# Prompt attention of a hybrid decoder step: score products as three rounded products, sampled pages in four slots

## The chip, the core and the metric

One program runs on one core of a Trainium2 chip. The core has a matrix engine (PE; its weight loads are listed apart as PEld), a vector engine (DVE), a scalar engine (ACT), a third elementwise engine (POOL) and a queue that issues transfers (SP). Each engine works through its own list of instructions in order, and the lists meet only at semaphores. The metric is the time of one execution on the device in microseconds (us), as the median of several runs.

## What is computed

One layer of inference for a prompt of 1024 tokens and for 8 sampled sequences of 4 new tokens each, with 4096 past tokens in pages. The change lies in the attention of the prompt. Eight query heads of 64 numbers share two key heads (KVH = 2, four queries each), and every query is scored against three sets of keys:

```python
qg = q.reshape(B, Tq, N_KV_HEADS, GROUP, HEAD_DIM).astype(F32) * (HEAD_DIM ** -0.5)
s = jnp.einsum('btkgd,bnkd->bkgtn', qg, cmp_kv[:, :, 0]) - slopes * d_c.astype(F32)      # compressed
p_cmp = masked_softmax(s, d_c >= 0)
...
s = jnp.einsum('btkgd,bktmd->bkgtm', qg, ksel) - slopes * d_s.astype(F32)                # selected
...
s = jnp.einsum('btkgd,bskd->bkgts', qg, win_kv[:, :, 0].astype(F32)) - slopes * d_w.astype(F32)   # window
...
o = g[:, :, 0] * o_cmp + g[:, :, 1] * o_slc + g[:, :, 2] * o_win
```

With 1024 tokens all 16 blocks are selected, so the selected branch of the prompt is attention over all earlier keys.

## The kernel before

The program has a `front` (projections, convolution, compression of the cache) and, behind a barrier, the stages `attend`, `out_projection`, two MLP stages and an embedding stage. The change touches `attend` alone, from 525 to 866 us of the profiled execution.

**Units.** The prompt's attention is cut into 32 units, one for each of 4 query groups g and 8 blocks i of 128 queries (`UNITS[n] = (g, i)`, so i is n modulo 8). A unit's scores are products of `c.q[rows, g, ...]` (64 rows of one head, 128 queries) with 64 (compressed), 128(i+1) (selected) and 128(min(i,4)+1) (window) keys. `chunks_of` packs these pieces into chunks of at most 512 columns. For each piece two products are issued, for heads e = 0 and 1, that is on rows 0 to 63 and 64 to 127 of the array, and they write two banks (line 1895). Chunks of the first two units are already made in `front`.

**The path of a unit.** PE multiplies a chunk (L1895); DVE adds the distance penalty and takes the extreme of each row (L2156, one instruction for each piece and head, with a read of the accumulator behind it); ACT exponentiates (L2043); DVE inverts the sums (L2166, in `weigh`); POOL scales by that and by the gate (L1862, six instructions for a unit); PE turns the weights, 128 columns at a time (L1907); ACT and DVE by turns copy the turned banks (L2052, L2170); PE multiplies with the values (L1919); ACT copies a unit's output to `mixA` (`keep_o`, L2066).

**Order.** The orders of all engines are written out by hand over 88 steps of one to four per unit. In a step of unit n, PE turns two groups of unit n, then issues the share of unit n+2's chunks that falls in the step, then the value products of the step before, then work of the sampled queries, which runs in 18 quads: turning keys (L1946), their scores (`quad_scores`, L1954) and values (L1982). PE's products write two pairs of banks by turns (`score_banks`): a job waits until DVE has read the job two before it, and prompt chunks and quad scores count alike as jobs. In a unit's first step ACT's `keep_o(n - 1)` stands behind the exponentials of the step before; it waits for `pv_done`, the last value product of unit n-1, which PE issues behind this step's score products. DVE's first step of a unit is: copies of turned banks, then the scores of unit n+2's chunks, then the quad's scores; `weigh(n + 1)` stands in the second step, or in the first where a unit has one step (i = 0).

**Pages.** SP loads the sampled pages in 36 halves of 1 MB into five slots `s_raw`; half h waits until the values of quad (h - 5) // 2 are multiplied. The first weights of `out_projection` wait for the values of quad NZ - 3.

Of the kernel before, what the change touches and what calls it, by code (L numbers as in the profile page):

```python
# [14 lines left out]
ALU = mybir.AluOpType  # L15
ACT = mybir.ActivationFunctionType
# [6 lines left out]
P = 128  # L23
# [1619 lines left out]
EARLY_EXPS = 12  # L1643
RAW_PLACE = (AREA + 8192, RAW_OFF, HIY_OFF, HIY_OFF + 8192, AREA)


def attend(c, ps):
# [10 lines left out]

    raw = [c.at(f"s_raw{s}", [P, 8, 256], F32, RAW_PLACE[s]) for s in range(5)]
    KT_ = [c.at(f"s_KT{s}", [P, QK_], F32, PT_OFF + 8192 + 2048 * s) for s in range(4)]  # L1660
# [139 lines left out]
    iotas, step = c.sem("s_iotas"), c.sem("s_dve_step")  # L1800
    raw_loaded = [c.sem(f"s_raw_loaded{s}") for s in range(5)]
    cmp_ready, cmp_exp, imp_ready, selected = c.sem("s_cmp_max"), c.sem("s_cmp_exp"), c.sem("s_imp_ready"), c.sem("s_selected")
# [7 lines left out]
    def page(h, bb, j):  # L1810

        return raw[h % 5][:, 4 * (bb % 2) + j, :]

    def on_sp(sp):
        for h in range(2 * NZ):
            z = h // 2
            if h >= 5:
                sp.wait_ge(t_done, turn_no["o", (h - 5) // 2] + 1)
            for bb in (2 * (h % 2), 2 * (h % 2) + 1):
                b = GRP * group_of(z) + bb  # L1820
                if place(z) == 0:
                    sp.dma_start(raw[h % 5][:, 4 * (bb % 2):4 * (bb % 2) + 4, :], win[b]).then_inc(raw_loaded[h % 5], 16)
                else:
                    _, pages = nc.values_load_multi_w_load_instructions(
                        c.pages[0:1, ds(b * NPG + 4 * (place(z) - 1), 4)], engines=[mybir.EngineType.SP], min_val=0, max_val=N_POOL - 1)
                    for j in range(4):
                        sp.dma_start(page(h, bb, j), cache[ds(pages[j], 1)].rearrange("o t f -> (o t) f")).then_inc(raw_loaded[h % 5], 16)

# [39 lines left out]
    def on_pe(pe):  # L1868
# [17 lines left out]
        def qk(n, ch):  # L1886
            g, i = UNITS[n]
            s = score_banks(("p", n, ch))
            off = 0
            for br, k0, w in CHUNKS[n][ch]:  # L1890
                for e in range(KVH):
                    rows = slice(DH * e, DH * e + DH)
                    w0 = P * max(0, i - 4)
                    keys = c.KcP[rows, :] if br == 0 else c.proj[rows, KS, k0:k0 + w] if br == 1 else c.proj[rows, KW, w0 + k0:w0 + k0 + w]
# [136 lines left out]
    def on_act(act):  # L2031
# [36 lines left out]
        def quad_exps(z):  # L2068
# [54 lines left out]
    def on_dve(dve):  # L2123
# [118 lines left out]
        def keep_out(gr):  # L2242
# [1562 lines left out]
```

## Time and profile before

| | us |
|---|---|
| median of 3 runs | 1786.9 (1786.52 to 1790.64) |
| the profiled execution, its own time | 1786.75 |
| its span in the trace | 1785.1 |
| stage `attend` within it | 525 to 866 |

PE is busy for 1729.3 us of the span, and in every other stage it is close to fully busy. In `attend` its work is in short bursts of four kinds, with idle gaps between them. A busy PE is not PE at its peak, since products are pipelined: what a burst costs is read from the start of one burst to the start of the next. The granted clock of PE is at its upper level (2.4 GHz) over nearly the whole span; a window that prints 0.50 had the lower one (1.2 GHz).

### The profile page before, as it was taken

What the parts mean: (1) busy time and instruction counts of PE and PEld (TensorE: products, weight loads), DVE (VectorE), ACT (ScalarE), POOL (GpSimd) and SP (SyncE); (2) the same over time, 40 slices, a digit from 0 to 9 for tenths busy, and PEclk for the clock granted to TensorE, in tenths of its full rate; (3) what the DMA queues carried; (4) which work ended last, traced back from release to release, by engine and by line L of the source; (5) the groups of instructions that cost most, each with busy time, mean ns of one, the idle gap of its engine ahead of it and who ended that gap; (6) DMA issues with size and microseconds to landing.
All of it is one profiled execution on the core that took longest, in us unless ns stands there. A gap on an engine that the chain in (4) does not pass through costs nothing.

```text
span 1785.1 us, 36056 instructions
## 1 busy us (share of the span) xinstructions
PE 1729.3 (97%) x13587; PEld 1603.5 (90%) x13587; DVE 1215.0 (68%) x1813; ACT 803.4 (45%) x1458; POOL 844.0 (47%) x862
## 2 busy tenths in 40 slices
PE   8999999999989999999998899999999999999998
PEld 7999999999876766676998899999999999999998
DVE  6789964878677677767647645555587878855535
ACT  5312323555766566666525233333443333314426
POOL 2203964545524343344444656566665555325531
PEclk9999997999999999999999999999999999999999
DMA  4421356545522544343314233222393733431214
GB/s 160 131 72 38 95 161 155 149 142 148 179 71 82 149 121 127 109 136 90 134 36 151 84 112 117 97 109 97 132 312 122 216 113 107 146 112 55 59 36 145
DMA packets 179723, 214.61 MB, mean 120 GB/s; under 512 B 22940, under 2 KB 150664, under 8 KB 174799
## 3 DMA queue, kind: packets, MB, share of 16 engines
q1 hardware_dynamic: 174461, 196.82, 35.5%
q0 software_dynamic: 4032, 13.40, 2.4%
q10 hardware_dynamic: 1058, 2.10, 0.4%
q8 instruction: 108, 1.77, 0.4%
q14 instruction: 64, 0.52, 0.1%
HBM read 181.30 MB, written 35.59 MB: 121 GB/s over the span
## 4 chain that ended last, share of the span: by engine, by line
PE 55%; DVE 8%; issue 3%; POOL 2%; ACT 2%; DMA 0%; ACTq 0%; SPq 0%; DVEq 0%; POOLq 0%
PE ps L2740 11%; PE ps L3123 7%; PE ps L2745 6%; PE ps L2500 5%; PE ps L3128 4%; PE ps L200 3%; PE ps L1907 3%; PE ps L3636 3%; PE ps L1919 3%; PE ps L1895 3%; POOL S L1862 2%; PE ps L1946 2%; DVE S L2156 2%; PE ps L206 2%; PE ps L3646 1%
## 5 line engine op out<-in xcount | busy, mean ns | idle before, releaser
L1862 POOL TENSOR_SCALAR S<-S,inv,gate_p 128x640 f32<-128x640 f32 (+7 forms) x186 | 124.9, 691 | 193.7 <-DVE inv L2166 193.7
L1260 DVE SCALAR_TENSOR_TENSOR y<-u,conv_w,y 128x1024 f32<-128x1024 f32 x120 | 156.4, 1349 | 1.2
L3123 PE MATMUL ps<-dn_op_hi,dn_hi 128*128 128x264 f32 x672 | 136.5, 285 | 2.9 <-DVE dn_op_lo L3171 2.9
L3123 PE MATMUL ps<-dn_op_lo,dn_hi 128*128 128x264 f32 x672 | 135.7, 283 | 0.0
L636 POOL COPY relaid<-raw 128x512 f32<-128x512 f32 x128 | 82.3, 675 | 94.9 <-PE ps_p L1034 35.6
L2043 ACT ACTIVATE S<-S,mn 128x64 f32<-128x64 f32 (+8 forms) x180 | 108.7, 609 | 2.1 <-DVE mn L2156 2.1
L3054 POOL TENSOR_TENSOR dn_lo<-dn_t_sum,dn_hi 128x512 fp32r<-128x512 f32 x48 | 76.4, 1592 | 66.7 <-ACT dn_hi L3076 66.5
L2740 PE MATMUL ps<-s_hi,up_hi 128*128 128x264 f32 x512 | 104.8, 286 | 3.0 <-ACT rstd L2710 3.0
L3123 PEld LDWEIGHTS ps<-dn_op_hi,dn_hi 128*128 128x128 f32 x672 | 103.7, 188 | 4.2 <-DVE dn_op_lo L3171 4.2
L963 PE MATMUL ps_p<-Ahi,win_hi 128*128 128x352 f32 x456 | 103.8, 327 | 1.5 <-DVE Alo L1237 1.5
L2740 PE MATMUL ps<-s_lo,up_hi 128*128 128x264 f32 x512 | 104.5, 286 | 0.0
L3123 PEld LDWEIGHTS ps<-dn_op_lo,dn_hi 128*128 128x128 f32 x672 | 103.9, 188 | 0.0
L963 PE MATMUL ps_p<-Alo,win_hi 128*128 128x352 f32 x456 | 103.5, 326 | 0.0
L1907 PEld LDWEIGHTS ps<-ident,S 128*128 128x128 f32 x592 | 64.9, 142 | 38.9 <-issue 21.0
L1907 PE MATMUL ps<-ident,S 128*128 128x128 f32 x592 | 86.4, 283 | 12.4 <-POOL S L1862 8.6
L1108 PE MATMUL ps_p<-Xhi,w1hi 128*128 128x256 f32 (+1 forms) x288 | 95.8, 333 | 1.0 <-ACT gT L772 0.8
L3128 PE MATMUL ps<-dn_op_hi,dn_lo 128*128 128x264 f32 x672 | 95.6, 284 | 0.0
L2610 POOL TENSOR_TENSOR up_lo<-up_sum,up_hi 128x512 fp32r<-128x512 f32 x48 | 70.5, 1469 | 46.6 <-ACT up_hi L2656 46.6
L3128 PEld LDWEIGHTS ps<-dn_op_hi,dn_lo 128*128 128x128 f32 x672 | 87.7, 188 | 0.0
L1110 PE MATMUL ps_p<-Xhi,w1lo 128*128 128x256 f32 (+1 forms) x288 | 84.7, 294 | 0.0
L1109 PE MATMUL ps_p<-Xlo,w1hi 128*128 128x256 f32 (+1 forms) x288 | 84.6, 294 | 0.0
L2740 PE MATMUL ps<-a_hi,up_hi 128*128 128x264 f32 x384 | 79.0, 288 | 5.6 <-DVE tmp L2817 3.5
(484 smaller groups left out, 5073.9 us busy)
## 6 DMA issues: line engine op xcount, KB each, us to landing
s_raw<-in_cache_slc_kv_dram SPq DMA_DIRECT2D x256, 128.0 KB, 2.1
raw<-in_cache_cmp_kv_dram SPq DMA_DIRECT2D x192, 128.0 KB, 3.1
dn_op_raw<-hidden SPq DMA_DIRECT2D x21, 1056.0 KB, 6.7
hidden<-cs SPq DMA_DIRECT2D x32, 528.0 KB, 2.6
up_raw<-in_w_up_dram SPq DMA_DIRECT2D x16, 1024.0 KB, 5.3
dn_w<-in_w_down_dram SPq DMA_DIRECT2D x48, 256.0 KB, 4.9
win_raw<-in_w_in_dram SPq DMA_DIRECT2D x38, 256.0 KB, 3.3
raw<-in_cache_cmp_kv_dram POOLq DMA_DIRECT2D x64, 128.0 KB, 2.6
```

Source lines behind the costliest of these rows:

```text
L963: mm = nc.tensor.matmul(ps[t % 2][:, j, 0:CH], w[t % 2][:, k, :], x[:, k, CH * j:CH * j + CH], start=(m == 0), stop=(m == NG - 1))
L1108: nc.tensor.matmul(out, w1hi[cc][:, at, :], x_hi, start=first, stop=False)
L1110: mm = nc.tensor.matmul(out, w1lo[cc][:, at, :], x_hi, start=False, stop=last)
L1260: i = V_.scalar_tensor_tensor(out=y, in0=x, scalar=w, in1=y, op0=ALU.mult, op1=ALU.add)
L1862: nc.gpsimd.tensor_scalar(x, x, inv[:, n % 3, 3 * e + br:3 * e + br + 1], c.gate_p[:, i, H * br + h:H * br + h + 1], ALU.mult, ALU.mult).t ...
L1907: mm = nc.tensor.transpose(ps[:, P * (2 * j + e):P * (2 * j + e) + P], S[UNITS[n][1]][:, e, col:col + P], c.ident[:])
L2043: nc.scalar.activation(x, x, ACT.Exp, bias=mn[:, n % 3, e, br, part:part + 1], scale=-1.0, accum_out=sums[:, n % 3, 3 * e + br:3 * e + br ...
L2500: mm = nc.tensor.matmul(banks[t % 2][:, j, 0:CH], w[t % 2][:, k, :], x(k)[:, CH * j:CH * j + CH], start=(n == 0 and m == 0), stop=(n == KT ...
L2740: nc.tensor.matmul(ps[:, bank + j, 0:HC], w_hi[s % 4][:, k, :], ops[m][:, k, c0 + HC * j:c0 + HC * j + HC], start=(k == 0 and m == 0), sto ...
L2745: mm = nc.tensor.matmul(ps[:, bank + j, 0:HC], w_lo[s % 4][:, k, :], ops[0][:, k, c0 + HC * j:c0 + HC * j + HC], start=False, stop=(k == K ...
L3123: nc.tensor.matmul(ps[:, 2 * m + j, 0:HC], w_hi[q % 4][:, k, :], x[:, k, HC * j:HC * j + HC], start=(k == 0 and x is op_hi[n]), stop=False)
L3128: mm = nc.tensor.matmul(ps[:, 2 * m + j, 0:HC], w_lo[q % 4][:, k, :], op_hi[n][:, k, HC * j:HC * j + HC], start=False, stop=(k == KH - 1))
```

## The change

Queries, keys and compressed keys are split into a part rounded to the format fp32r (`hi`, a copy on ACT) and the rest (`lo`, a subtraction on DVE). Each score piece becomes three products that add up in the bank, hi by hi, hi by lo and lo by hi, in place of one product of fp32 numbers. The keys are split at the start of the stage, in two parts cut at column 384. Queries are split unit by unit: unit 2's at the start, and in the first step of unit n those of unit n+3. `K_hi` takes the place of the fifth page slot, so there are four: half h waits for the values of quad (h - 4) // 2, and the weights of `out_projection` for quad NZ - 2.

```diff
-RAW_PLACE = (AREA + 8192, RAW_OFF, HIY_OFF, HIY_OFF + 8192, AREA)
+RAW_SLOTS = 4
+RAW_PLACE = (HIY_OFF, RAW_OFF, HIY_OFF + 8192, AREA + 8192)
+KEY_CUT = 384
...
+    K_hi = c.at("K_hi", [P, 2, T], F32R, AREA)
+    K_lo = c.at("K_lo", [P, 2, R], F32R, PROJ_OFF + 4 * R * KS)
+    KcP_hi = c.at("KcP_hi", [P, 64], F32R, RSTD_OFF + 4096)
+    KcP_lo = c.at("KcP_lo", [P, 64], F32R, B1_OFF + 15616)
+    q_lo = c.at("q_lo", [P, PAIRS, R], F32R, U_OFF)
+    q_hi = [sb("q_hi0", [P, P], F32R), c.at("s_q_hi1", [P, P], F32R, RSTD_OFF + 3584)]
+    query_part = lambda n: 1 if n == 2 else n + 2
...
-            if h >= 5:
-                sp.wait_ge(t_done, turn_no["o", (h - 5) // 2] + 1)
+            if h >= RAW_SLOTS:
+                sp.wait_ge(t_done, turn_no["o", (h - RAW_SLOTS) // 2] + 1)
...
+            if ch == 0:
+                pe.wait_ge(part_lo, 3 if n == 2 else query_part(n))
+            w0 = P * max(0, i - 4)
+            hi, lo = q_hi[n % 2], q_lo[query(n)]
             for br, k0, w in CHUNKS[n][ch]:
-                for e in range(KVH):
-                    rows = slice(DH * e, DH * e + DH)
-                    ...
-                    mm = nc.tensor.matmul(ps_S[:, s + e, off:off + w], c.q[rows, g, P * i:P * i + P], keys, start=True, stop=True)
+                for m, (x, split, compressed) in enumerate(((hi, K_hi, KcP_hi), (hi, K_lo, KcP_lo), (lo, K_hi, KcP_hi))):
+                    for e in range(KVH):
+                        rows = slice(DH * e, DH * e + DH)
+                        mm = nc.tensor.matmul(ps_S[:, s + e, off:off + w], x[rows, :], keys(rows, split, compressed), start=(m == 0), stop=(m == 2))
...
+        def query_high(n):
+            if n >= 4:
+                act.wait_ge(qk_done, score_no["p", n - 2, len(CHUNKS[n - 2]) - 1] + 1 - len(EARLY))
+            nc.scalar.activation(q_hi[n % 2][:], c.q[query(n)], ACT.Copy).then_inc(part_hi, 1)
+        query_high(2)
+        nc.scalar.activation(K_hi[:, :, KEY_PARTS[0]], c.proj[:, KS:KW + 1, KEY_PARTS[0]], ACT.Copy).then_inc(part_hi, 1)
...
                 if j == 0 and n:
                     keep_o(n - 1)
+                if j == 0 and n + 3 < NU:
+                    query_high(n + 3)
...
-                    if k == 0:
-                        act.wait_ge(t_done, turn_no["o", NZ - 2] + 1)
+                    if k < 2:
+                        act.wait_ge(t_done, turn_no["o", NZ - 2 + k] + 1)
...
+        def query_low(n):
+            dve.wait_ge(part_hi, query_part(n))
+            V_.tensor_tensor(q_lo[query(n)], c.q[query(n)], q_hi[n % 2][:].bitcast(F32), ALU.subtract).then_inc(part_lo, 1)
...
                 z = quad_at(st, 1)
                 if z is not None:
                     keep_keys(z, 3)
+                if j == 0 and n + 3 < NU:
+                    query_low(n + 3)
...
-    c.t_done, c.slot_free = t_done, turn_no["o", NZ - 3] + 1
+    c.t_done, c.slot_free = t_done, turn_no["o", NZ - 2] + 1
```

The changed file's lines stand some 30 further down. DVE in the first step of unit 12, before: a copy of a turned bank and of keys, then unit 14's scores (`S_10086`) and the quad's (`s_S`).

```order
L2170 COPY PT_10091<-ps 128x512
L2173 COPY s_KT_10101<-ps 128x512
L2156 ISA S_10086,mn<-ps,far_selected,neg_slope 128x512
...
L2156 ISA S_10086,mn<-ps,far_selected,mn,neg_slope 128x384
...
L2156 ISA S_10086,mn<-ps,far_compressed,neg_slope 128x64
L2156 ISA mn 128x1
L2207 ISA s_S_10102,s_mx<-ps,s_S_10102,s_mx 128x512
```

The same place after the change:

```order
L2202 COPY PT_10091<-ps 128x512
L2205 COPY s_KT_10105<-ps 128x512
L2285 TENSOR_TENSOR q_lo<-q_back,s_q_hi_10132 128x128
L2188 ISA S_10086,mn<-ps,far_selected,neg_slope 128x512
L2188 ISA mn 128x1
...
L2239 ISA s_S_10106,s_mx<-ps,s_S_10106,s_mx 128x512
```

The subtraction for unit 15's queries has moved in ahead of unit 14's scores. It waits for this row of ACT's list, `s_q_hi`, which stands behind the output copy `mixA` (`keep_o`) of the same step:

```order
L2064 ACTIVATE S_10085,sums<-S_10085,mn 128x640 x2
L2087 ACTIVATE mixA<-ps 128x128
L2104 ACTIVATE s_q_hi_10132<-q_back 128x128
L2073 ACTIVATE PT_10088<-ps 128x512
L2098 ACTIVATE s_alpha<-s_mx,s_nm,row_slope 128x1
```

In unit 8, whose only step also holds `weigh(9)`, the subtraction stands ahead of the inversion as well:

```order
L2202 COPY PT_10089<-ps 128x256
L2205 COPY s_KT_10105<-ps 128x512
L2285 TENSOR_TENSOR q_lo<-q_back,s_q_hi_10132 128x128
L2198 RECIPROCAL inv<-sums 128x6
L2188 ISA S_10082,mn<-ps,far_selected,neg_slope 128x384
```

PE's list has, for the first chunk of unit 2 with 384 and 64 columns, six products where there were two for each piece:

```order
L1916 MATMUL ps<-K_hi,q_lo 128x384 x2
L1916 MATMUL ps<-KcP_hi,s_q_hi_10131 128x64 x2
L1916 MATMUL ps<-KcP_lo,s_q_hi_10131 128x64 x2
L1916 MATMUL ps<-KcP_hi,q_lo 128x64 x2
L1916 MATMUL ps<-K_hi,s_q_hi_10131 128x384 x2
```

These rows are its last product with selected keys, its three with compressed ones and the first of the next chunk; each "x2" is the two heads.

## Rows read from the trace of the kernel before

**Rows 1.** Stage attend by window: start:end, length, busy us (count), clock, DMA.
```profile
525.00:866.00 341.00, 322.73 (x3464) 228.49 (x3466) 242.23 (x806) 219.49 (x600) 146.96 (x217) 0.99 0.40 119
```

**Rows 2.** Line L1895: ns min/median/max, first and last start, forms and counts.
```profile
L1895 PE MATMUL ps<-proj,q_back x368: 269/538/1006, 526.5 to 847.2; 64*128 64x512 f32 x80, 64*128 64x128 f32 x44, 64*128 64x384 f32 x32, 64*128 64x256 f32 x28
L1895 PE MATMUL ps<-KcP,q_back x120: 216/272/418, 527.9 to 847.3; 64*128 64x64 f32 x120
```

**Rows 3.** Timeline, bursts on PE and weight loads: start, us, engine, line, shapes, count.
```profile
646.32 1.13 PE L1895 MATMUL ps<-proj,q_back 64*128 64x512 f32 x4
647.38 1.09 PE L1919 MATMUL ps<-PT,V 128*64 128x128 f32 x16
...
663.58 1.99 PE L1895 MATMUL ps<-proj,q_back 64*128 64x512 f32 x8
665.50 0.66 PE L1919 MATMUL ps<-PT,V 128*64 128x128 f32 x8
...
642.89 0.92 PE L1895 MATMUL ps<-proj,q_back 64*128 64x256 f32 x8
643.92 1.09 PE L1919 MATMUL ps<-PT,V 128*64 128x128 f32 x16
...
664.12 0.19 PEld L1895 LDWEIGHTS ps<-proj,q_back 64*128 64x128 f32 x2 [0.24 <-issue]
```

**Rows 4.** Timeline, rounded products of front, 132 columns wide.
```profile
264.05 0.28 PE L1108 MATMUL ps_p<-Xhi,w1hi 128*128 128x132 f32 x1
264.16 0.27 PE L1109 MATMUL ps_p<-Xlo,w1hi 128*128 128x132 f32 x1
```

**Rows 5.** Timeline, unit 12's first step (brackets: idle before it, releaser).
```profile
653.73 0.28 ACT L2066 ACTIVATE mixA<-ps 128x128 f32<-128x128 f32 x1 [0.47 <-PE ps L1919]
...
654.03 1.06 PE L1954 MATMUL ps<-s_KT,QB 128*32 128x512 f32 x8 [0.35 <-DVE mn L2156]
```

**Rows 6.** Timeline, unit 9.
```profile
625.61 0.26 ACT L2066 ACTIVATE mixA<-ps 128x128 f32<-128x128 f32 x1
...
625.80 0.19 DVE L2166 RECIPROCAL inv<-sums 128x6 f32<-128x6 f32 x1 [0.42 <-ACT S L2043]
...
626.10 3.36 POOL L1862 TENSOR_SCALAR S<-S,inv,gate_p 128x384 f32<-128x384 f32 x6 [5.65 <-DVE inv L2166]
```

**Rows 7.** Timeline, unit 16.
```profile
706.35 0.18 DVE L2166 RECIPROCAL inv<-sums 128x6 f32<-128x6 f32 x1
...
707.39 0.28 ACT L2066 ACTIVATE mixA<-ps 128x128 f32<-128x128 f32 x1 [0.74 <-PE ps L1919]
```

**Rows 8.** Timeline, unit 13 (its third job starts at the second row).
```profile
666.42 0.28 ACT L2066 ACTIVATE mixA<-ps 128x128 f32<-128x128 f32 x1 [0.96 <-PE ps L1919]
...
667.33 1.13 PE L1895 MATMUL ps<-proj,q_back 64*128 64x512 f32 x4
```

**Rows 9.** Groups by form in attend: busy us, mean ns of one, idle before it.
```profile
L2156 DVE CUSTOM_DVE_ANT_0 S<-ps,far_selected,neg_slope 128x512 f32<-128x512 f32 x40 | 28.4, 748 | 11.0 <-PE ps L1895 10.9
...
L2066 ACT ACTIVATE mixA<-ps 128x128 f32<-128x128 f32 x31 | 8.4, 270 | 14.3 <-PE ps L1919 14.3
L2112 ACT ACTIVATE y_hi<-y 128x1056 fp32r<-128x1056 f32 x4 | 4.3, 1076 | 0.0
L2295 DVE TENSOR_TENSOR y_lo<-y,y_hi 128x1056 fp32r<-128x1056 f32 x4 | 5.3, 1328 | 0.2 <-ACT y_hi L2112 0.2
```

**Rows 10.** Timeline at the start of the stage: PE's wait for DVE.
```profile
530.12 0.62 PE L1930 MATMUL ps<-KcS,QB 128*32 128x256 f32 x2 [0.59 <-DVE mn L2156]
```

**Rows 11.** Window with half the clock, a burst of turns in it, and another elsewhere.
```profile
551.00:553.00 2.00, 2.00 (x10) 1.72 (x9) 0.29 (x1) 1.29 (x3) 0.69 (x2) 0.50 0.00 0
...
551.21 1.91 PE L1946 MATMUL ps<-ident,s_raw 128*128 128x128 f32 x8
...
631.60 1.09 PE L1946 MATMUL ps<-ident,s_raw 128*128 128x128 f32 x8
```

**Rows 12.** Timeline, pages issued on SP's queue.
```profile
599.82 10.46 SPq L1827 DMA_DIRECT2D s_raw<-in_cache_slc_kv_dram  x12
```

More of the change, by code:

```diff
@@ L1657, in attend @@
     LOW = 1e20
-    raw = [c.at(f"s_raw{s}", [P, 8, 256], F32, RAW_PLACE[s]) for s in range(5)]
+    raw = [c.at(f"s_raw{s}", [P, 8, 256], F32, RAW_PLACE[s]) for s in range(RAW_SLOTS)]
+    K_hi = c.at("K_hi", [P, 2, T], F32R, AREA)
[3 more added lines that the diff above has]
+    q_lo = c.at("q_lo", [P, PAIRS, R], F32R, U_OFF)
     KT_ = [c.at(f"s_KT{s}", [P, QK_], F32, PT_OFF + 8192 + 2048 * s) for s in range(4)]
@@ L1793, in attend @@
     HALF_DMAS = lambda h: 2 if place(h // 2) == 0 else 8
-    arrived = lambda h: 16 * sum(HALF_DMAS(x) for x in range(h % 5, h + 1, 5))
+    arrived = lambda h: 16 * sum(HALF_DMAS(x) for x in range(h % RAW_SLOTS, h + 1, RAW_SLOTS))
     qk_done, score_read = c.sem("qk_done"), c.sem("score_read")
@@ L1800, in attend, with query @@
     iotas, step = c.sem("s_iotas"), c.sem("s_dve_step")
-    raw_loaded = [c.sem(f"s_raw_loaded{s}") for s in range(5)]
+    raw_loaded = [c.sem(f"s_raw_loaded{s}") for s in range(RAW_SLOTS)]
+    part_hi, part_lo = c.sem("key_or_query_hi_ready"), c.sem("key_or_query_lo_ready")
+    query_part = lambda n: 1 if n == 2 else n + 2
+    KEY_PARTS = (slice(0, KEY_CUT), slice(KEY_CUT, T))
+    def query(n):
+        g, i = UNITS[n]
+        return (slice(None), g, slice(P * i, P * i + P))
     cmp_ready, cmp_exp, imp_ready, selected = c.sem("s_cmp_max"), c.sem("s_cmp_exp"), c.sem("s_imp_ready"), c.sem("s_selected")
@@ L1810, in page @@
     def page(h, bb, j):
-        return raw[h % 5][:, 4 * (bb % 2) + j, :]
+        return raw[h % RAW_SLOTS][:, 4 * (bb % 2) + j, :]
     def on_sp(sp):
@@ L1826, in on_sp @@
                     for j in range(4):
-                        sp.dma_start(page(h, bb, j), cache[ds(pages[j], 1)].rearrange("o t f -> (o t) f")).then_inc(raw_loaded[h % 5], 16)
+                        sp.dma_start(page(h, bb, j), cache[ds(pages[j], 1)].rearrange("o t f -> (o t) f")).then_inc(raw_loaded[h % RAW_SLOTS], 16)
     def on_pool(pool):
@@ L1889, in qk, with keys @@
             off = 0
+            if ch == 0:
+                pe.wait_ge(part_lo, 3 if n == 2 else query_part(n))
+            w0 = P * max(0, i - 4)
+            hi, lo = q_hi[n % 2], q_lo[query(n)]
             for br, k0, w in CHUNKS[n][ch]:
-                for e in range(KVH):
-                    rows = slice(DH * e, DH * e + DH)
-                    w0 = P * max(0, i - 4)
-                    keys = c.KcP[rows, :] if br == 0 else c.proj[rows, KS, k0:k0 + w] if br == 1 else c.proj[rows, KW, w0 + k0:w0 + k0 + w]
-                    mm = nc.tensor.matmul(ps_S[:, s + e, off:off + w], c.q[rows, g, P * i:P * i + P], keys, start=True, stop=True)
+                def keys(rows, split, compressed):
+                    return compressed[rows, :] if br == 0 else split[rows, 0, k0:k0 + w] if br == 1 else split[rows, 1, w0 + k0:w0 + k0 + w]
+                for m, (x, split, compressed) in enumerate(((hi, K_hi, KcP_hi), (hi, K_lo, KcP_lo), (lo, K_hi, KcP_hi))):
+                    for e in range(KVH):
+                        rows = slice(DH * e, DH * e + DH)
+                        mm = nc.tensor.matmul(ps_S[:, s + e, off:off + w], x[rows, :], keys(rows, split, compressed), start=(m == 0), stop=(m == 2))
                 off += w
@@ L1941, in turn_keys @@
             h = 2 * z + half
-            pe.wait_ge(raw_loaded[h % 5], arrived(h))
+            pe.wait_ge(raw_loaded[h % RAW_SLOTS], arrived(h))
             for bb in (2 * half, 2 * half + 1):
@@ L2078, in quad_exps @@
             nc.scalar.activation(Ss[z % 2][:], Ss[z % 2][:], ACT.Exp, bias=shift, scale=slope, accum_out=part_sum[:, z % 2, 0:1]).then_inc(sx_done, 1)
+        def query_high(n):
[4 more added lines that the diff above has]
+        nc.scalar.activation(K_hi[:, :, KEY_PARTS[0]], c.proj[:, KS:KW + 1, KEY_PARTS[0]], ACT.Copy).then_inc(part_hi, 1)
+        nc.scalar.activation(KcP_hi[:], c.KcP[:], ACT.Copy).then_inc(part_hi, 1)
+        nc.scalar.activation(K_hi[:, :, KEY_PARTS[1]], c.proj[:, KS:KW + 1, KEY_PARTS[1]], ACT.Copy).then_inc(part_hi, 1)
         late = []
@@ L2249, in keep_out @@
             o.then_inc(kept[1], 1)
+        def query_low(n):
+            dve.wait_ge(part_hi, query_part(n))
+            V_.tensor_tensor(q_lo[query(n)], c.q[query(n)], q_hi[n % 2][:].bitcast(F32), ALU.subtract).then_inc(part_lo, 1)
+        query_low(2)
+        dve.wait_ge(part_hi, 2)
+        V_.tensor_tensor(K_lo[:, :, KEY_PARTS[0]], c.proj[:, KS:KW + 1, KEY_PARTS[0]], K_hi[:, :, KEY_PARTS[0]].bitcast(F32), ALU.subtract).then_inc(part_lo, 1)
+        dve.wait_ge(part_hi, 3)
+        V_.tensor_tensor(KcP_lo[:], c.KcP[:], KcP_hi[:].bitcast(F32), ALU.subtract).then_inc(part_lo, 1)
+        dve.wait_ge(part_hi, 4)
+        V_.tensor_tensor(K_lo[:, :, KEY_PARTS[1]], c.proj[:, KS:KW + 1, KEY_PARTS[1]], K_hi[:, :, KEY_PARTS[1]].bitcast(F32), ALU.subtract).then_inc(part_lo, 1)
         dve.wait_ge(iotas, 7)
```

2 lines of the change are left out of this document (1 added, 1 removed).

## The prediction, made before the changed kernel had run

> **What bounds the kernel now.** I read the windows first, by stages. PE is near full everywhere, and in attend it is busy for 322.73 of 341 us, DVE for 242, ACT for 219, POOL for 147 [rows 1]. So a microsecond of PE's work taken away in attend is worth nearly one, as long as PE doesn't then wait for somebody. The idle 18.3 us of PE shows that it already waits: the timeline has PE held by DVE's reading of scores [rows 5] and POOL by DVE's inversion [rows 6]. The stage is a loop through all engines, and what matters next to PE's work is how soon DVE reads a unit's scores.
>
> **What the products cost.** The line of the score products has 488 records, four for each piece (two heads, two passes of an fp32 product); by the forms there are 40 pieces of 512 columns, 16 of 384, 14 of 256, 22 of 128 and 30 of 64 [rows 2]. One chunk of 512 takes PE from 646.32 to 647.38, 1.06 us; two in a row take from 663.58 to 665.50, 1.92 us. So 512 columns cost 0.86 us and the burst as such 0.20 us. 0.86 us is 2048 periods of 2.4 GHz, four a column for both heads together: four records stream 1024 periods each, so the two heads run at the same time, and so do their weight loads (two in 0.19 us, the time of one) [rows 3]. A chunk of 256, 128 and 64 columns takes 1.03 us, 0.83 without the burst; 384 columns are 0.64 of that, so the 64 columns are about 0.17 [rows 3].
>
> **What three rounded products cost.** The fp32 pass streams two periods a column. Rounded products of 132 columns, each with its own load of 128 columns of weights, start 0.11 us apart, though 132 periods are 0.055 us [rows 4]. So I take for a pass of both heads the larger of one period a column and 0.107 us. Three passes then cost 0.64 us for 512 columns (saves 0.21), 0.48 for 384 (0.16), 0.32 for 256 (0.11), 0.32 for 128 (before 0.21, loses 0.11) and 0.32 for 64 (before 0.17, loses 0.15). Sum: 40 x 0.21 + 16 x 0.16 + 14 x 0.11 - 22 x 0.11 - 30 x 0.15 = 8.4 + 2.6 + 1.5 - 2.4 - 4.5 = **5.6 us saved on PE**; I write 6, as a 64-column piece may load its first weights under the piece before. The bound above is that loads hide wholly: 34944 columns less one period each of four, 14.6 us, some 13 with a few ns per product. The bound below is the rival of serial heads.
>
> The Trainium skill, FP8 and Floating Point Precision, TensorE Precision Notes, says that a true fp32 product makes four passes through the array. The trace's four periods a column agree. By that rule alone three passes for four would save the whole 14.6 us; the rows on short rounded products speak against it, and by them 6.
>
> **What is moved, and who waits.** 28 queries are split unit by unit. The copy on ACT and the subtraction on DVE are short: an ACT copy of 128 columns takes 0.27 us, and DVE needs 1.33 us for 1056 columns, so 0.16 us in proportion and up to 0.3 with a fixed share; I take 0.25 [rows 9]. In all some 8 us more on ACT and 7 us on DVE, beside a stage of 341 us in which neither is full: by itself nothing.
>
> Their place is what costs. In a unit's first step ACT rounds the query behind `keep_o(n - 1)`, which waits for PE's last value product of unit n-1; that stands on PE behind this step's score products. DVE's `query_low(n + 3)` waits for ACT, and queued behind it on DVE are the reading of the scores just multiplied, in the one-step units also the inversion for the next unit. Nothing needs q_lo(n+3) before the next unit: the wait serves nobody, but it holds DVE until 0.28 + 0.27 + 0.25 = 0.80 us after the start of `keep_o`. For `keep_o` the trace has 14.3 us of idle time ended by PE in 31 copies: it follows the value product directly in many of them, else the exponentials of the step before [rows 9]. Before, DVE reads scores as soon as the chunk is multiplied, mostly 1.5 to 3 us sooner.
>
> I went through the 28 starts of units in the timeline, adding 0.80 us to `keep_o` and 0.71 us for each 512-column piece and head (28.4 us for 40) [rows 9], up to the first thing on PE that needs it:
> - *Five starts with a quad's scores in the step* (units 8, 12, 18, 20, 26). The quad's product needs the bank of the job two before it. Unit 12: DVE is free at 653.73 + 0.80 = 654.53, has read the first chunk at 655.95, and PE's product started at 654.03 [rows 5]: 1.9 us. Five make 10.
> - *Four second units of a query group* (1, 9, 17, 25), where two chunks of 512 lie between the split and the inversion. Unit 9: 625.61 + 0.80 + 4 x 0.71 = 629.25, and the inversion was at 625.80, with POOL idle 5.65 us for it and PE's turning right behind [rows 6]: 3.4. The four make 2.9 + 3.4 + 1.1 + 3.0 = 10.4.
> - *Two one-step units* (16, 24). Unit 16: the inversion stood at 706.35 and comes at 707.39 + 0.80 = 708.19 [rows 7]: 1.8. Together 4.
> - *Nine starts in which PE's third job or a bank of turned blocks comes too late* (2, 5, 6, 10, 13, 14, 21, 22, 28). Unit 13: 666.42 + 0.80 + 1.42 = 668.64 against 667.33 [rows 8]: 1.3. By the same reckoning these are 0.2 to 2.7 each, together 15.
> - *The other eight* (3, 4, 7, 11, 15, 19, 23, 27) have other work on PE or short scores: 3.
>
> Sum 42 us. Some of it falls into gaps that PE has already: of its 18.3 us idle [rows 1] I take 10 off, **32 us** for this term. Its bounds are 21 (half of the sum, if DVE and ACT catch up and the stalls of neighbours overlap) and 42.
>
> **The start of the stage.** Before PE's first score product ACT now rounds a query, 768 columns of keys and 64 compressed ones (0.27 + 0.8 + 0.2 us, the keys by proportion of 1.08 us for 1056), and DVE subtracts (1.0 + 0.15 behind it) [rows 9]; the second key part of 1280 columns adds 1.3 us on ACT and 1.6 on DVE ahead of their first copies and the first scores. DVE reads them about 1.4 us later than now, and PE's product at 530.12 already waits for DVE [rows 10]. With the lower clock held a little longer: **2 us**.
>
> **Clock.** At 551.00:553.00 the granted clock was 0.50, the lower level, and a burst of eight turns took 1.91 us, against 1.09 us for such a burst elsewhere [rows 11]. New pauses of 2 to 3 us may bring more such stretches. I take none into the sum and 5 us (six at 0.8) into the upper bound. The Trainium skill, TensorE: Matmul & The Clock Gate, HAM oscillation, says that idle gaps between bursts bring the lower clock back, which speaks against this change; by that row such a stretch costs 0.8 us a burst.
>
> **Slots.** The even half of a quad's pages now starts a quad later. Twelve transfers take SP 10.46 us [rows 12], so the 16 of a quad 14 us, the first eight 7; between the values that free the slots and the turning of the keys lie 4 to 6 steps of 3.9 us (341 for 88). The first half has 15 us or more for 7, the second 19 for 14: hidden. If transfers took twice as long it would be late by some 7 us a quad.
>
> **Sum.** 1786.75 (the profiled execution, 0.15 under the median of 1786.9, so no correction) + 32 + 2 - 6 = 1814.75: **1815 us**, 1.6% slower.
>
> **The rivals.**
> - *Faster: the wait is hidden and PE's saving stays.* It decides whether PE's other work between the last value product and the next consumer of a bank (turning, keys, sampled values) is longer than 0.80 us plus the reading, 2.2 us. It is in unit 15 and a few more, not in units 8, 9 or 12. If it were nearly everywhere, 1786.75 + 2 - 6 to - 13: 1776 to 1783, middle 1781. For it: DVE is idle for 99 of 341 us. Against it: the rows of units 9, 12 and 13.
> - *Nothing measurable.* Stalls of a third of the sum, 14 us, with the full saving of 13 and 2 for the start: about 1788.
> - *Heads in turn.* No row shows rounded products on half the rows. If the two heads' products did not run together, a pass would cost twice: six periods a column instead of four, 34944 x 2 / 2.4 GHz = 29 us more instead of 6 less. With the stalls partly covered: 1840 to 1850. For it: nothing but the missing row; against: the fp32 products on the same halves do overlap [rows 3].
>
> **How the numbers follow.** Chances: the forecast 0.70, heads in turn 0.12, nothing measurable 0.08, faster 0.10. A measurement of this kernel can tell about 0.3% (5.4 us) from no change. Faster by more 0.10, within 0.08, slower 0.82. The forecast's own bounds: 1786.75 + 21 + 1 - 13 = 1796, and 1786.75 + 42 + 2 + 5 - 0 = 1836. Taking in part of the washed-out case below and of heads in turn above, the range is 1790 to 1842; outside are the faster case and small parts of the two.
>
> **What would show it.** After the change: bursts of 512 columns on PE of about 0.85 us, not 1.06 (the saving) and not 1.5 (heads in turn); 64- and 128-column pieces no faster than before. On DVE the new subtraction as one of the largest waits, ended by ACT, 28 times for 1 to 3 us, and PE's idle time for DVE's reads and POOL up from 18 to 40 us or more in a stage of some 370 us; everything behind the stage as before. The forecast is wrong if DVE's subtraction waits less than 0.5 us on average, or if PE's idle time in the stage stays near 18 us.

## The result, and the profile after

| | before | after |
|---|---|---|
| median | 1787.4 us (1786.5 to 1790.6, 4 runs) | 1839.5 us (1837.1 to 1844.7, 4 runs) |
| ratio, 95% interval | | 1.0287 (1.0263 to 1.0312) |
| the profiled execution | 1786.75 | 1839.03 |
| first score product of the stage, in its span | 526.47 | 529.78 |
| first product of `out_projection` | 866.50 | 917.64 |

The change makes the kernel 2.9% slower, by 52 us. 1815 was predicted, 28 us more than before, with 1790 to 1842 around it. The two windows between those points, of before and of after (columns: length, then busy time and instruction count of PE, PEld, DVE, ACT and POOL, the granted clock, the share of the DMA engines and GB/s):

```profile
526.47:866.50 340.03, 321.79 (x3466) 227.68 (x3465) 242.73 (x806) 219.67 (x600) 146.06 (x209) 0.99 0.40 120
```

```profile
529.78:917.64 387.86, 335.80 (x3708) 254.13 (x3708) 247.25 (x836) 225.98 (x629) 146.59 (x209) 0.94 0.35 105
```

The stage takes 47.8 us more. PE's idle time in it, length less busy, goes from 18.2 to 52.1 us (+33.8), and PE's busy time rises by 14.0 us although the products were to become cheaper. Of the 52.3 us by which the spans differ, 3.3 lie before the first score product and 1.2 behind the stage. Counted from PE's first product of the stage (525.03 before, 527.42 after), 2.4 of the 3.3 lie ahead of the stage and 0.9 in it: the first score product comes 2.36 us behind that product instead of 1.44, since it waits for the split of the keys:

```profile
529.78 0.69 PE L1916 MATMUL ps<-K_hi,s_q_hi 64*128 64x384 f32 x2 [0.84 <-DVE KcP_lo L2291]
```

**The wait.** From the list of waits of after (engine and line, what it waited for, us in total, times, longest):

```profile
POOL S L1878 <- DVE inv L2198: 241.0, 30, 12.5
ACT PT L2073 <- PE ps L1928: 105.2, 59, 8.0
DVE q_lo L2285 <- ACT s_q_hi L2104: 70.7, 29, 5.2
```

DVE's new subtraction waits 70.7 us for ACT's copy. PE's part of the list has no such line; there the same wait appears as waits for `mn`, what DVE's readings of scores write, for `s_KT`, DVE's copies of keys, and for POOL:

```profile
PE ps L1928 <- POOL S L1878: 14.0, 15, 2.2
PE ps L1975 <- DVE mn L2188: 11.4, 5, 2.5
PE ps L1916 <- DVE mn L2188: 9.4, 8, 2.0
PE ps L1967 <- DVE s_KT L2205: 5.8, 4, 3.0
```

Before, PE waited 8.6 us for POOL in the first of these lines, 1.8 us in the second, none in the third and 1.1 us in the fourth.

The timeline of unit 12 shows the whole chain (start, duration, engine, line, output<-input, idle time before it and what ended it), the place of [rows 5]:

```profile
678.30 0.44 PE L1940 MATMUL ps<-PT,VcP 128*64 128x128 f32 x4
...
678.78 0.28 ACT L2087 ACTIVATE mixA<-ps 128x128 f32<-128x128 f32 x1 [0.27 <-PE ps L1940]
678.96 0.30 ACT L2104 ACTIVATE s_q_hi<-q_back 128x128 fp32r<-128x128 f32 x1
679.29 0.29 DVE L2285 TENSOR_TENSOR q_lo<-q_back,s_q_hi 128x128 fp32r<-128x128 f32 x1 [1.87 <-ACT s_q_hi L2104]
679.50 0.75 DVE L2188 CUSTOM_DVE_ANT_0 S<-ps,far_selected,neg_slope 128x512 f32<-128x512 f32 x1
...
680.98 1.06 PE L1975 MATMUL ps<-s_KT,QB 128*32 128x512 f32 x8 [2.24 <-DVE mn L2188]
```

PE ends its value products, ACT copies the output and then rounds the query, DVE subtracts, and only then reads the first 512 columns twice; PE's next product waits for the second reading, 2.24 us.

**The bursts.** The same piece of 512 columns as in [rows 3], now in three passes, from the first row to the start of the next kind of work:

```profile
683.00 0.50 PE L1916 MATMUL ps<-K_hi,s_q_hi 64*128 64x512 f32 x2
683.34 0.40 PE L1916 MATMUL ps<-K_lo,s_q_hi 64*128 64x512 f32 x2
683.57 0.41 PE L1916 MATMUL ps<-K_hi,q_lo 64*128 64x512 f32 x2
683.90 1.09 PE L1940 MATMUL ps<-PT,V 128*64 128x128 f32 x16
```

0.90 us instead of 1.06. By size, at full clock: 512 columns 1.06 to 0.89, two of 512 1.92 to 1.59, 384 0.85 to 0.72, 256 0.63 to 0.55, but 128 0.42 to 0.48 and 64 0.37 to 0.45.

**The clock.** The granted clock falls to its lower level, 1.2 GHz, much more often. This is the row behind PE's pause of unit 16, and the two-us windows there (the clock stands third from the end):

```profile
740.62 2.18 PE L1928 MATMUL ps<-ident,S 128*128 128x128 f32 x8 [2.19 <-POOL S L1878]
```

```profile
738.00:740.00 2.00, 0.42 (x8) 0.18 (x4) 1.02 (x5) 0.47 (x2) 0.53 (x1) 1.00 0.79 234
740.00:742.00 2.00, 1.26 (x6) 0.87 (x7) 2.00 (x11) 0.40 (x1) 2.00 (x6) 0.71 0.35 90
742.00:744.00 2.00, 2.00 (x10) 1.47 (x10) 1.90 (x6) 2.00 (x10) 1.38 (x3) 0.50 0.69 201
744.00:746.00 2.00, 2.00 (x22) 1.32 (x21) 0.92 (x2) 1.32 (x6) 0.00 (x0) 0.94 0.00 0
```

Summed over all such windows from 524 on (2 us for one at 0.50, in proportion for the others) the lower level holds for 51 us, against 8.5 before. Of that, 47 and 6 lie behind the first score product.

### The profile page after: what moved, and what is told of

Read it like the earlier page. It is cut to its first block, busy times and chain, and to the rows that moved or that the text cites. A ratio compares the mean times of both kernels' runs of the same rounds, so it can differ in the third digit from the quotient of the medians.

```text
span 1837.4 us, 36639 instructions
## 1 busy us (share of the span) xinstructions
PE 1745.4 (95%) x13831; PEld 1631.5 (89%) x13831; DVE 1222.5 (67%) x1846; ACT 811.4 (44%) x1491; POOL 843.7 (46%) x862
## 4 chain that ended last, share of the span: by engine, by line
PE 48%; DVE 10%; issue 5%; ACT 4%; POOL 2%; DMA 1%; SPq 0%; ACTq 0%; DVEq 0%; POOLq 0%
PE ps L2785 11%; PE ps L3168 6%; PE ps L2790 5%; PE ps L2545 4%; PE ps L3173 3%; PE ps L200 3%; PE ps L1928 2%; PE ps L1916 2%; PE ps L1940 2%; DVE S L2188 2%; PE ps L3681 2%; POOL S L1878 2%; PE ps L206 1%; DVE dn_op_lo L3216 1%; ACT S L2064 1%
## 5 line engine op out<-in xcount | busy, mean ns | idle before, releaser
L1928 PE MATMUL ps<-ident,S 128*128 128x128 f32 x592 | 91.4, 294 | 20.2 <-POOL S L1878 14.0
L2073 ACT ACTIVATE PT<-ps 128x512 f32<-128x512 f32 (+1 forms) x80 | 45.0, 562 | 105.4 <-PE ps L1928 105.2
```

What stands on the lines that cost most here:

```text
L1928: mm = nc.tensor.transpose(ps[:, P * (2 * j + e):P * (2 * j + e) + P], S[UNITS[n][1]][:, e, col:col + P], c.ident[:])
```

## The experiments

For each profile the table gives the stage from its first score product to the first product of `out_projection`, PE's busy and idle time in it, and the time at the lower clock, summed from 2-us windows from 524 on. These four columns are of one execution each; medians and ratios are of all. Ratios are to the kernel before on the same chip.

| kernel | median, us | ratio (95%) | stage | busy | idle | lower clock |
|---|---|---|---|---|---|---|
| before | 1787.4 | 1 | 340.0 | 321.8 | 18.2 | 8.5 |
| after | 1839.5 | 1.0287 (1.0263 to 1.0312) | 387.9 | 335.8 | 52.1 | 51.1 |
| e4_four_slots | 1790.8 | 1.0010 (0.9997 to 1.0023) | 340.3 | 322.1 | 18.3 | 10.2 |
| e3_wait_alone | 1838.8 | 1.0272 (1.0245 to 1.0300) | 391.5 | 340.2 | 51.4 | 47.8 |
| e1_split_early | 1790.3 | 1.0012 (1.0001 to 1.0023) | 339.5 | 319.9 | 19.7 | 17.1 |
| e2_subtraction_late | 1792.1 | 1.0019 (1.0010 to 1.0029) | 341.1 | 320.0 | 21.1 | 17.1 |
| e7_copy_early | 1788.7 | 1.0011 (1.0000 to 1.0022) | 338.9 | 318.5 | 20.3 | 12.0 |
| e5_pauses_filled | 1834.2 | 1.0257 (1.0236 to 1.0277) | 380.6 | 336.6 | 44.0 | 27.3 |
| e8_two_products | 1783.8 (one run) | not timed | 329.7 | 300.0 | 29.6 | 17.1 |
| e6_compressed_fp32 | 1791.0 | 1.0009 (0.9999 to 1.0019) | 339.9 | 316.6 | 23.3 | 16.8 |
| e9_keys_later | 1791.8 | 1.0014 (1.0004 to 1.0023) | 342.4 | 318.4 | 24.0 | 13.7 |
| e10_both | 1791.8 | 1.0012 (1.0001 to 1.0022) | 339.5 | 315.1 | 24.4 | 13.4 |

The first score product starts anywhere from 525.5 to 532.3 in these profiles, though the code ahead of the stage is the same in all. So of the 3.3 us by which it is later in the profile of after only the 0.9 within the stage say something of the change. They stand in every version that splits all keys at the start (2.36 us from PE's first product of the stage to its first score product), and are absent in e4_four_slots and e3_wait_alone (1.44). The column "stage" leaves them out. With them, from PE's first product of the stage to the first of `out_projection`, it is 341.5 us before, 390.2 after, 341.8 in e4_four_slots and 341.9 in e1_split_early.

### The two parts of the change apart: the slots, and the wait

e4_four_slots, from the kernel before:

```diff
-RAW_PLACE = (AREA + 8192, RAW_OFF, HIY_OFF, HIY_OFF + 8192, AREA)
+RAW_SLOTS = 4
+RAW_PLACE = (HIY_OFF, RAW_OFF, HIY_OFF + 8192, AREA + 8192)
```

e3_wait_alone, from e4_four_slots, with the copy on ACT and the subtraction on DVE where the changed kernel has them:

```diff
                 if j == 0 and n:
                     keep_o(n - 1)
+                if j == 0 and n + 3 < NU:
+                    query_high(n + 3)
...
                     keep_keys(z, 3)
+                if j == 0 and n + 3 < NU:
+                    query_low(n + 3)
```

> The kernel before with the sampled pages in four slots, and nothing else of the change. My theory: the loads are hidden, 1785 to 1789 us, no wait of PE's turning of keys over 1 us in the stage. Rival (the first half of a quad comes late by a part of the 2.4 us of the front or by some us a quad): 1790 or more, with PE's key turning waiting for the queue.

> The kernel before, with its fp32 products and unsplit keys, with four slots and with the 28 query copies on ACT and subtractions on DVE in the places of the changed kernel; their results are read by nobody. My theory: the wait alone brings pauses and clock, so the time is that of the changed kernel with 5 us more on PE and without the longer start: 1786.75 + 35 + 20 = 1830 to 1848, PE idle 48 to 56 us in the stage, 40 us or more at the lower clock, DVE's subtraction waiting 60 to 80 us. Rival (the clock falls because of the rounded products): 1786.75 + 35 = about 1822, with under 15 us at the lower clock. Second rival (the wait is not the cause): 1787 to 1795.

Four slots cost nothing that can be told: the ratio's interval holds 1, and the stage is 0.3 us longer (the median is above the 1785 to 1789 that I gave, but so was that of the kernel before beside it, 1789.2). The wait alone, with the old products, gives the whole loss: 1.0272 against 1.0287, with intervals that overlap. Its time, idle time, lower clock and waits all lie in what was expected. The few us by which the old products are dearer don't show in the medians; its four executions lie between 1834 and 1841 us. From the waits of e3_wait_alone:

```profile
DVE q_lo_unused L2269 <- ACT s_q_hi L2092: 73.5, 28, 4.8
```

The stages of e4_four_slots and of e3_wait_alone, same columns as above:

```profile
529.20:869.53 340.33, 322.06 (x3466) 227.08 (x3465) 242.82 (x806) 219.62 (x600) 146.10 (x209) 0.99 0.40 120
```

```profile
528.33:919.86 391.53, 340.18 (x3466) 235.33 (x3465) 245.32 (x835) 226.47 (x629) 145.38 (x209) 0.94 0.35 104
```

PE executes the same 3466 instructions in both. Idle time rises by 33.1 us, and the same work takes 18.1 us longer, with 37.6 us more at the lower clock: 0.48 us for each. Together 51.2 us. So the lower clock comes with the pauses and not from rounded products, of which this kernel has none in its scores; nor from the split of the keys, which it doesn't have either.

### Without the wait

e1_split_early, from the changed kernel, on ACT (the line goes to the head of the step) and on DVE (it goes to the end of the step):

```diff
+                if j == 0 and n + 3 < NU:
+                    query_high(n + 3)
                 for k in steps[st]:
...
                 if j == 0 and n:
                     keep_o(n - 1)
-                if j == 0 and n + 3 < NU:
-                    query_high(n + 3)
...
-                if j == 0 and n + 3 < NU:
-                    query_low(n + 3)
...
+                if j == 0 and n + 3 < NU:
+                    query_low(n + 3)
```

> The changed kernel with the query's copy at the head of ACT's step (ahead of the exponentials and keep_o) and the subtraction at the end of DVE's step (behind the readings of scores); the products, keys and slots are as changed. My theory (the wait of DVE's subtraction for the copy is what costs: 35 us of pauses on PE, and some 20 us of lower clock that follow the pauses): DVE's subtraction waits under 3 us in all instead of 70.7, PE's idle time in the stage is 18 to 22 us instead of 53, the time at the lower clock falls from 50 to 10 to 15 us, and the kernel takes 1783 to 1791 us. Rival (the rounded products themselves, or the split of the keys, bring the lower clock; the wait costs only its own pauses): 1839 less 35 = 1804, with 40 us or more still at the lower clock. Second rival (four slots or the work of the split hold PE): over 1815.

e2_subtraction_late moves the line on DVE alone, e7_copy_early the one on ACT alone.

> The changed kernel with one line moved: DVE's subtraction of the query stands at the end of DVE's step, behind the readings of scores; ACT's copy stays behind keep_o. My theory (what costs is only what is queued behind the waiting subtraction on DVE): as e1_split_early, 1786 to 1793, with DVE's subtraction waiting under 5 us. Rival (ACT's copy behind keep_o itself delays ACT's next exponentials, which PE's turning needs): 1795 to 1805.

> The changed kernel with the other line moved alone: ACT's copy of the query stands at the head of ACT's step, ahead of the exponentials and keep_o; DVE's subtraction stays ahead of the readings of scores. My theory (the wait is for keep_o, which waits for PE's last value product): DVE waits for ACT only where ACT is late by its exponentials, under 15 us in all, and the kernel takes 1787 to 1797. Rival (DVE would wait at that place for whatever ACT has in hand, so half of the cost stays): 1805 to 1820, with 30 us or more of waits.

Each of the three takes the loss away. The place of unit 12 in e1_split_early:

```profile
651.24 0.30 ACT L2104 ACTIVATE s_q_hi<-q_back 128x128 fp32r<-128x128 f32 x1
654.03 0.75 DVE L2188 CUSTOM_DVE_ANT_0 S<-ps,far_selected,neg_slope 128x512 f32<-128x512 f32 x1 [0.21 <-PE ps L1916]
...
655.17 0.28 ACT L2087 ACTIVATE mixA<-ps 128x128 f32<-128x128 f32 x1 [0.27 <-PE ps L1940]
...
655.51 1.06 PE L1975 MATMUL ps<-s_KT,QB 128*32 128x512 f32 x8 [0.39 <-DVE mn L2188]
```

DVE reads the scores 1.1 us before the output copy instead of 0.7 behind it, and PE's pause is 0.39 us, not 2.24. PE's idle time of 19.7 us in the stage lies in the range told, the time at the lower clock of 17.1 us a little above it. DVE's subtraction waits for ACT 1.9 us in all here. With either line moved alone it is (e2_subtraction_late, where under 5 us was expected, then e7_copy_early):

```profile
DVE q_lo L2285 <- ACT s_q_hi L2104: 6.1, 7, 1.9
```

```profile
DVE q_lo L2285 <- ACT s_q_hi L2104: 2.7, 3, 1.9
```

Both rivals fell: the copy behind `keep_o` by itself delays nothing much, and DVE doesn't wait for whatever else ACT has in hand. It was the dependence on `keep_o`, that is on PE, and what stood behind it on DVE.

But none of the three beats the kernel before; all lie 0.1 to 0.2% above it, within what I called no change. The stage of e1_split_early:

```profile
528.41:867.95 339.54, 319.87 (x3709) 245.46 (x3709) 250.19 (x836) 225.55 (x629) 146.50 (x209) 0.98 0.40 120
```

Against e4_four_slots PE is busy 2.2 us less, with 6.9 us more at the lower clock, at 0.48 each 3.3 us: the products save 5.5 us, of which 3.3 go to the lower clock and 1.4 into idle time. The lower clock lies in the first stretch of the stage in both, up to 552 here and up to 557 there. The 0.8 us that are left are used up by the first score product, which comes 0.9 us later: nothing reaches the end of the stage.

### Is the lower clock caused by the pauses?

```diff
 e5_pauses_filled, from the changed kernel
+FILLED = (1, 8, 10, 12, 16, 18, 20, 21, 24, 26)
...
                 for k in (steps[st - 1] if st else ()):
                     pv(k)
+                if j == 0 and n in FILLED:
+                    pe.wait_ge(o_kept, n)
+                    nc.tensor.matmul(ps_O[:, 0:512], c.ident[:], c.Tslc[:, 0:512], start=True, stop=True)
```

> The changed kernel with one fp32 product of 512 columns more on PE (0.86 us, read by nobody) behind the last value product and keep_o in ten of the units, those where PE then pauses for 2 us or more. It separates the pauses' own length from the lower clock that follows them. My theory (the clock falls behind long pauses, and a pause cut in two keeps it): the time at the lower clock falls from 50 to 25 to 35 us (what the start and the stretch at 545 to 560 hold stays), and the kernel takes 8 to 12 us less than the changed one less up to 4 us for the fillers: 1829 to 1836. Rival (the clock follows how much PE has to do over a longer stretch, so single fillers change nothing): 1839 to 1848, with 45 us or more at the lower clock.

Ten products of which nobody reads anything make the kernel 5 us faster by the medians; the intervals of the two ratios still overlap (the executions lie at 1832.5 to 1837.8 and at 1837.1 to 1844.7). The stage, one execution of each, is 380.6 us against 387.9. Unit 16 again, PE's rows and then the windows, to be held against the four windows of after above:

```profile
738.16 1.13 PE L2034 MATMUL ps<-far_selected,ident 128*128 128x512 f32 x2 [0.38 <-ACT mixA L2091]
739.98 0.66 PE L1929 MATMUL ps<-ident,S 128*128 128x128 f32 x4 [0.69 <-POOL S L1879]
741.05 0.66 PE L1929 MATMUL ps<-ident,S 128*128 128x128 f32 x4 [0.42 <-POOL S L1879]
```

```profile
738.00:740.00 2.00, 1.15 (x3) 0.32 (x3) 1.66 (x9) 0.30 (x2) 1.17 (x3) 1.00 0.63 199
740.00:742.00 2.00, 1.58 (x12) 1.13 (x14) 1.93 (x9) 1.33 (x4) 2.00 (x5) 1.00 0.47 137
742.00:744.00 2.00, 2.00 (x24) 1.36 (x20) 1.97 (x5) 2.00 (x9) 0.75 (x1) 1.00 0.38 125
```

One pause of 2.19 us has become three of 0.38, 0.69 and 0.42, and the clock stays at 1.00. Over the stage the time at the lower clock falls from 51.1 to 27.3 us; this and the time of the kernel lie in what was expected. Busy time rises by 0.8 us, though the fillers take 11.3, so the other work takes 10.5 less; 23.8 us times 0.48 is 11.4. Idle time falls by 8.1 us, since the fillers lie in it. A filler shortens a pause and gives PE more to do at once, so this run doesn't tell which of the two keeps the clock up. What is left at the lower clock is the start, 528 to 542, and stretches at 552 to 562 and 648 to 651.

The Trainium skill, TensorE: Matmul & The Clock Gate, HAM oscillation, says that idle gaps between bursts send the clock back, so that the next burst starts at the lower one. These two runs agree: the same work takes 18.1 us longer in e3_wait_alone, and all but the fillers 10.5 us less in e5_pauses_filled. The page's example is one of waits for DMA; here it was pauses of 2.0 to 3.0 us, in which PE waited for DVE and POOL.

### What a pass costs, and what PE's time is worth

e8_two_products is e1_split_early without the third product, so its scores lack the low part of the query.

```diff
-                for m, (x, split, compressed) in enumerate(((hi, K_hi, KcP_hi), (hi, K_lo, KcP_lo), (lo, K_hi, KcP_hi))):
+                for m, (x, split, compressed) in enumerate(((hi, K_hi, KcP_hi), (hi, K_lo, KcP_lo))):
```

> The kernel of e1_split_early with two products instead of three (the product of the query's low part with the keys' high part is left out, so the scores lack that term). It measures what one pass costs by size. My theory (a pass of both heads costs the larger of one period a column and 0.107 us): a 512-column burst falls from 0.89 to 0.68 us, a 256-column one from 0.55 to 0.44, 128 from 0.48 to 0.37, 64 from 0.45 to 0.34; 34944 columns and the 52 short pieces make 40 x 0.213 + 16 x 0.16 + 66 x 0.107 = 18 us less PE work in the stage than e1. Rival (the short pieces cost a fixed start and end that does not depend on the number of passes): 64 and 128 columns fall by under 0.05 us.

```profile
643.24 0.51 PE L1916 MATMUL ps<-K_hi,s_q_hi 64*128 64x512 f32 x2
643.58 0.39 PE L1916 MATMUL ps<-K_lo,s_q_hi 64*128 64x512 f32 x2
643.90 0.66 PE L1940 MATMUL ps<-PT,V 128*64 128x128 f32 x8
```

0.66 us for 512 columns. A pass of both heads costs 0.23 us for 512 columns, 0.17 to 0.18 for 384, 0.12 for 256 and 0.11 for 128 and for 64. That is the model of the prediction, one period a column but no less than a floor, with some 0.02 us more for each long pass. The floor is the same for 128 and 64 columns; that it is the load of the weights is the prediction's reading, and no run here tests it. The rival of a fixed start and end fell.

The Trainium skill, FP8 and Floating Point Precision, TensorE Precision Notes, counts four passes for a true fp32 product. The 0.86 us for 512 columns before, four periods a column, agree. By that count three passes for four would have saved 14.6 us, an estimate; some 5 is what the runs show, since a pass over 128 or 64 columns costs the floor and not its columns.

PE has 19.8 us less to do than in e1_split_early (18 expected), and the stage is 9.9 us shorter; the other 9.9 are idle. The same shows at a smaller size in three variants meant to beat both kernels:

e6_compressed_fp32, from e1_split_early:

```diff
+                if br == 0:
+                    for e in range(KVH):
+                        ...
+                        mm = nc.tensor.matmul(ps_S[:, s + e, off:off + w], c.q[rows, g, P * i:P * i + P], c.KcP[rows, :], start=True, stop=True)
```

e9_keys_later, from e1_split_early, and e10_both, from e6_compressed_fp32, do the second part of the keys in the first step, on ACT ahead of `keep_o` and on DVE behind the subtraction of the query:

```diff
-        nc.scalar.activation(K_hi[:, :, KEY_PARTS[1]], c.proj[:, KS:KW + 1, KEY_PARTS[1]], ACT.Copy).then_inc(part_hi, 1)
...
+                if st == 0:
+                    nc.scalar.activation(K_hi[:, :, KEY_PARTS[1]], c.proj[:, KS:KW + 1, KEY_PARTS[1]], ACT.Copy).then_inc(part_hi, 1)
```

> e1_split_early with the compressed keys (pieces of 64 columns) multiplied as fp32 again, from the unsplit query, and so without the split of the compressed keys at the start; the query's low parts stand in two buffers used in turn. My theory (a short piece costs more in three rounded passes, 0.45 against 0.36 us alone, and e1 lost its 5 us of saved PE work again by some 4 us of lower clock and 3 us more idle): 30 pieces x 0.09 = 2.7 us less PE work than e1 and 0.2 to 0.4 us less at the start, of which half reaches the end: 1786 to 1789, ratio to before 0.997 to 1.000. Rival (changing between the two kinds of product inside a chunk costs as much as it saves): as e1, 1790, or 1 to 3 us above it.

> e1_split_early with the second part of the keys (1280 columns a partition) rounded and subtracted at the end of the first step instead of ahead of the first step. My theory (what is left of the change's cost is at the start, where DVE reads the first scores late and the lower clock lasts 17 us instead of 10): the first readings come 1.3 to 1.6 us sooner, the lower clock lasts 8 to 13 us, and the kernel takes 1785 to 1788.5, ratio 0.997 to 1.000. Rival (the 1.6 us on DVE hold the readings of the second step instead, so the pause only moves): as e1, 1789 to 1791.

> e6_compressed_fp32 with the second part of the keys split at the end of the first step too. My theory: as e9, and 1 us less for the short pieces: 1784 to 1788. Rival (PE is no longer what bounds the stage, so neither is worth anything): 1789 to 1791.

All three expectations were too good. e6_compressed_fp32 takes 3.3 us off PE's busy time and adds 3.6 to its idle time. e9_keys_later has 3.4 us less at the lower clock, and 4.4 us more idle, of which 1.7 are a new wait of PE for the moved subtraction:

```profile
PE ps L1916 <- DVE K_lo L2338: 1.7, 1, 1.7
```

e10_both, with both edits, has 4.7 us less of PE's busy time than e1_split_early and 4.7 us more idle. No version here beats the kernel before.

## Why the prediction was right, and where it was not

Direction, mechanism and places were right. The sum was 24 us short, nearly all in one term. That the time still lies in the range is partly luck: the forecast's own bounds were 1796 to 1836, and 1839.5 is above them. The range reached to 1842 because a part of "heads in turn" was taken in, a rival that fell.

- **The stalls: 32 us predicted, 33.8 measured.** Idle time of PE from one `keep_o` to the next, before and after, by the prediction's own groups: the five starts with a quad +9.0 (10 predicted), the second units +7.0 (10.4), the one-step units +3.9 (4), the nine with a late third job or bank +9.0 (15), the other eight +4.7 (3). Most of the places came as told, but in two of the nine (2 and 22) nothing was lost. In unit 12, from one output copy to the next, it is the 2.95 us that PE's busy time leaves of the length (0.96 before):

```profile
678.78:693.05 14.27, 11.32 (x135) 8.19 (x136) 9.08 (x30) 8.15 (x22) 5.40 (x7) 1.00 0.38 108
```

The sum of the 28 is 33.4, where the prediction had 42 and took 10 off. Those 10 were a guess and not a reckoning; 9.4 of them are what two of its groups had too much. The 0.80 us from the start of `keep_o` to the end of the subtraction is 0.80 in unit 12 (678.78 to 679.58), though the three take 0.28, 0.30 and 0.29: they overlap. In unit 9 the inversion was put 3.64 us behind `keep_o`; it stands 3.63 behind it, and POOL's idle time goes from 5.65 us [rows 6] to 10.06:

```profile
643.40 0.26 ACT L2087 ACTIVATE mixA<-ps 128x128 f32<-128x128 f32 x1
...
647.03 0.19 DVE L2198 RECIPROCAL inv<-sums 128x6 f32<-128x6 f32 x1
647.32 1.94 POOL L1878 TENSOR_SCALAR S<-S,inv,gate_p 128x384 f32<-128x384 f32 x3 [10.06 <-DVE inv L2198]
```

- **The clock: 0 predicted, 5 at most, some 20 measured.** This is the step that failed. The prediction saw the lower level in [rows 11] and priced "such a stretch" at 0.8 us for one burst, six times. Stretches of 3.4 to 13.7 us came instead, 51 us in all, of which 43 are new; at 0.48 for each us some 20. It had reckoned 28 new waits of up to 3 us, said that they may bring more such stretches, and put nothing for that into the sum.
- **The products: 5.6 to 6 us predicted, some 5 measured:** 4.8 by the bursts of each kind and their counts, 5.5 by e1_split_early with the lower clock taken off. Bursts of 512 columns were to take 0.85 us and take 0.89; the short ones got dearer, as said. A small slip: 0.83 less 0.64 us is 0.19 for the 64 columns and not 0.17, worth 0.6 us over 30 pieces. The heads do not take turns: two products of one pass stand in one row of x2, and passes follow each other by 0.23 us.
- **The start: 2 us predicted, 0.9 seen at the first score product.** In the medians it is not resolved: with the wait gone, all that is left of the change is within 0.2%. In the traces of e1_split_early and e4_four_slots, from PE's first product of the stage, the first score product comes 0.92 us later, DVE's first reading 0.8 (1.0 in after, 1.4 predicted) and the first output copy 2.0. The lower clock of the first stretch lasts 7 us longer, which at 0.48 would be 3 us; it is part of the clock term above.
- **The slots: nothing predicted, nothing measured** (1.0010, 0.9997 to 1.0023).
- **The sum in the stage,** from its first score product: 33.8 idle + 20 clock - 5 products = 49, against 47.8 measured.
- **The rival "faster".** It would have given 1776 to 1783 if the wait were hidden. e1_split_early hides it and takes 1790. So that branch was mispriced: the start and the lower clock behind it take 4.2 us where it had 2, and 1.4 went into new waits. The sentence behind it, that a microsecond less of PE's work is worth nearly one, doesn't hold here. In e8_two_products it was worth half, in e6_compressed_fp32 nothing: the stage is a loop in which PE waits for POOL, ACT and DVE as soon as PE gets faster.

Of the signs named in advance, the large wait on DVE (29 times, 2.4 us on average), the idle time over 40 us and the bursts came as told; the stage is 388 us long and not 370, the clock being most of the difference.

## What to carry to other kernels

An instruction that nobody needs soon still stops whatever is queued behind it on its engine: ask of each new one not only what it waits for, but whether that leads back to the engine that bounds the stage. Where pauses on PE are reckoned, count the lower clock behind them as a term of its own, here 0.55 to 0.6 us for each us of new pause; a profile of before in which pauses are rare shows little of it. And before a saving on the busiest engine is put into a sum, ask how long the next engine of the loop lets it stay busy.

## What was not expected of the hardware

- Not every pause brings the lower clock. Behind the first stretch of the stage, eleven pauses of PE in the trace of after are 2.0 us or longer. Seven are followed by a stretch at 1.2 GHz, which begins at most 2.2 us behind the pause and once within it (they end at 544.18, 635.76, 657.64, 740.62, 781.50, 798.67 and 838.69), four are not (680.98, 714.21, 758.90 and 857.96), with lengths of 2.0 to 3.0 us in the one set and 2.0 to 2.2 in the other. In e3_wait_alone the pauses at three of those four places, as long to 0.01 us (2.24, 2.05 and 2.24 us, they end at 677.24, 711.69 and 759.60), are followed by it. And before the change it fell at 549.6, behind two pauses of 1.14 and 1.07 us. So neither the place nor the length of the one pause decides; what does stays open.
- The four executions of after differ by 7.6 us, and the clock goes with the time: the fastest, 1837.06 us, has a mean granted clock of 0.976, the slowest, 1844.69 us, one of 0.970.
- Work that nobody reads can be worth its time: ten fillers took 11.3 us of PE, and the stage of that execution was 7.3 us shorter.
